# A chunked RWKV block and two attention layers on one core: top-128 selection with scores behind each query unit, masks made by GpSimd, and a new order of the steps in both attentions

## What is computed

```python
def block(args):                      # 128 queries
    s = jnp.einsum('bqhd,bsd->bqhs', qib, ki) * IDX_DIM ** -0.5      # 8 index heads
    score = jnp.einsum('bqh,bqhs->bqs', wib, jax.nn.relu(s))
    score = jnp.where(vis[None], score, NEG_INF)
    _, idx = lax.top_k(score, k_top)                                  # k_top = 128
    ...
    logits = jnp.einsum('bqgrd,bqkgd->bqgrk', qg, ksel) * scale + bias
    p = jax.nn.softmax(logits, axis=-1)
    o = jnp.einsum('bqgrk,bqkgd->bqgrd', p, vsel)
```

## Time and profile before

| | before |
|---|---|
| median of 3 runs | 2185.52 us (2184.66 to 2186.93) |
| the profiled execution | 2186.16 us |
| its span, first to last instruction | 2184.9 us |
| mean granted TensorE clock | 0.991 |
| first attention with selection | 810 to 1095 us |
| second attention | 1560 to 1780 us |

### The profile page before, as it was taken

One profiled execution on the slowest core, in us unless ns is written; L12 is line 12 of the kernel. 1 busy time (PEld: TensorE's weight loads), 2 busy tenths in 40 slices (PEclk: granted clock), 3 DMA queues, 4 the chain that ended last, 5 costly groups with the idle time before them and its releaser, 6 DMA issues.

```text
span 2184.9 us, 45350 instructions
## 1 busy us (share of the span) xinstructions
PE 2128.2 (97%) x19810; PEld 1871.8 (86%) x19810; DVE 1465.8 (67%) x2482; ACT 993.9 (45%) x1735; POOL 126.0 (6%) x121
## 2 busy tenths in 40 slices
PE   8999999999999999889999999999999999999999
PEld 2877788888778889778889999999988899999987
DVE  5889888887796866855576676334666567676622
ACT  4225556565525353245454444224666654443311
POOL 0000000000000004233310000000000030000000
PEclk9999999999999999979999999999999999999999
DMA  7631021111332543100132322223211023222232
GB/s 292 129 113 50 10 83 46 46 46 46 126 97 87 164 138 116 32 11 23 37 124 88 94 91 85 88 99 127 68 40 30 25 87 103 92 92 88 90 100 72
DMA packets 60021, 184.26 MB, mean 84 GB/s; under 512 B 7184, under 2 KB 11280, under 8 KB 59824
## 3 DMA queue, kind: packets, MB, share of 16 engines
q1 hardware_dynamic: 59824, 181.37, 25.8%
HBM read 174.73 MB, written 6.62 MB: 83 GB/s over the span
## 4 chain that ended last, share of the span: by engine, by line
PE 84%; DVE 10%; ACT 3%; issue 1%; DMA 1%; POOL 0%; SPq 0%; DVEq 0%; ACTq 0%
PE PS L604 67%; PE PS L789 3%; PE PS L778 2%; DVE ca L2064 2%; PE PS L1150 2%; PE PS L1281 2%; PE PS L798 1%; PE PS L1249 1%; DVE Swk L2501 1%; DVE mx L2497 1%; ACT Lb L1329 1%; DVE wlo L1962 1%; PE PS L1123 1%; PE PS L769 1%; DMA early<-in_wall 1%
## 5 line engine op out<-in xcount | busy, mean ns | idle before, releaser
L604 PE MATMUL PS<-nhi,whi 128*128 128x264 f32 (+1 forms) x2064 | 432.3, 291 | 2.4 <-ACT Vk L1329 1.5
L604 PE MATMUL PS<-nhi,wlo 128*128 128x264 f32 (+1 forms) x2064 | 419.1, 285 | 1.5 <-DVE wlo L1962 1.5
L604 PE MATMUL PS<-nlo,whi 128*128 128x264 f32 (+1 forms) x2064 | 419.3, 285 | 0.0
L1329 ACT ACTIVATE whi<-raw 128x1024 fp32r<-128x1024 f32 (+3 forms) x322 | 306.5, 953 | 199.5 <-PE PS L604 199.5
L1962 DVE TENSOR_TENSOR wlo<-raw,whi 128x1024 fp32r<-128x1024 f32 (+1 forms) x260 | 311.5, 1205 | 99.4 <-ACT whi L1329 99.3
L604 PEld LDWEIGHTS PS<-nhi,whi 128*128 128x128 f32 x2064 | 321.9, 191 | 9.9 <-ACT Vk L1329 1.7
L604 PEld LDWEIGHTS PS<-nhi,wlo 128*128 128x128 f32 x2064 | 321.3, 190 | 1.8 <-DVE wlo L1962 1.7
L604 PEld LDWEIGHTS PS<-nlo,whi 128*128 128x128 f32 x2064 | 321.7, 190 | 0.0
L604 PE MATMUL PS<-hhi,whi 128*128 128x512 f32 x648 | 266.5, 411 | 0.7 <-DVE hlo L2017 0.4
L604 PE MATMUL PS<-hhi,wlo 128*128 128x512 f32 x648 | 255.1, 394 | 0.5 <-DVE wlo L1962 0.4
L604 PE MATMUL PS<-hlo,whi 128*128 128x512 f32 x648 | 253.5, 391 | 0.0
(11 more groups left out here) (390 smaller groups left out, 3486.0 us busy)
## 6 DMA issues: line engine op xcount, KB each, us to landing
raw<-in_wall SPq DMA_DIRECT2D x266, 512.0 KB, 3.5
early<-in_wall SPq DMA_DIRECT2D x16, 512.0 KB, 14.7
raw<-in_wall SPq DMA_DIRECT2D x16, 384.0 KB, 3.0
TZ<-g_rows SPq DMA_DIRECT2D x2, 2112.0 KB, 10.0
raw<-in_wall SPq DMA_DIRECT2D x32, 128.0 KB, 2.0
raw<-in_wall SPq DMA_DIRECT2D x16, 256.0 KB, 2.7
g_rows<-gsb SPq DMA_DIRECT2D x8, 328.0 KB
xt<-in_xT SPq DMA_DIRECT2D x2, 1024.0 KB, 8.7
```

The costliest lines, as they stand in the source:

```text
L604: q = e.matmul(out, cuts[a][:, k * P:(k + 1) * P], (hi_, lo_)[b][:, kr, lo:lo + w], start=start and k == 0 and a == b == 0, stop=stop and ...
L1329: return e.activation(out, src, func, **kw)
```

## The change

Five things. The index products and scores of a query unit are done for all four blocks right behind that unit (t outside, i inside), in other PSUM banks (`SCORE_BANKS`), with two halves of `rel` in turn. The rounds write LOW into the scores themselves, the 16th round replaces too, and block 0 takes two rounds on the reversed negative scores; with that the mask is one comparison by GpSimd, and `above`, `equal`, `ranks`, `picked` and the sum of the masks are gone, as is the wait of a block's rounds for the mask of the block ahead. The scaling of a head's queries moves from VectorE to GpSimd (both norm gains go into the keys). In both attentions the steps behind a block of 528 keys have a new order: the result of the step ahead is applied and copied before the turn (first attention) or copied ahead of the scaling (second). `SELECT` is written anew with `FIRST` 5, and in `BEFORE` the letter p moves ahead of three t.

```diff
-BEFORE = "fftttpftfftptffffpfftftfffttfpffpffffftf"
+BEFORE = "ffptttftfftptffffpfftftfffttfpffpffffftf"
-SELECT = ("g" * 16 + 3 * "gggsggdggg" + "gsggdgrgrgrgrgr" + "grgrgrsgrgrdggg" + "sgrgrdgrsgrdgggg" + "sgrgrdgrgrgggg"
...
-FIRST = 4
+FIRST = 5
+SELECT = ("ggggggggggggggggggsggdsggsgggsgsgssgggdddddggsgsdddgggggsgddggssdggsdsdsggdsggrgrgrrgrgg"
...
+SCORE_BANKS = {3: ((4, 5), (6, 7)), 2: ((4,), (5,)), 1: ((6,), (7,)), 0: ((4,), (5,))}
...
         def tensor(e):
-                for i in (3, 2, 1, 0):
-                    q0, nq, w = rows_of(i)
-                    wide = w > 512
-                    for t in range(4):
+                for t in range(4):
+                    for i in (3, 2, 1, 0):
+                        q0, nq, w = rows_of(i)
...
+                    first = rest_apart(steps, n - 2)
+                    if first and n > 2:
+                        apply(n - 3)
+                    if not first and 2 <= n <= N + 1:
                         turn(n - 2)
                     yield
-                    if 3 <= n <= N + 2:
+                    if first:
+                        turn(n - 2)
...
         def scalar(e):
+                steps = [(t, i) for t in range(4) for i in (3, 2, 1, 0)]
+                for n, (t, i) in enumerate(steps):
                     w = WIDTH[i]
-                    for t in range(4):
-                        first = (4, 6) if w > 512 or t % 2 == 0 else (5, 7)
-                        for n in range(2):
-                            h = 2 * t + n
-                            on.wait_ge(*at("index", i, h))
-                            if h >= 4 or i < 3:
-                                on.wait_ge(*at("score", i if h >= 4 else i + 1, (h - 4) % 8))
-                            act(sv(rel[:, h % 4, 0:w], w), psv(w, first[n]), ACT.Relu, scale=0.125).then_inc(*up("rel", i, h))
-                        yield
+                    for r in range(2):
+                        h = 2 * t + r
+                        on.wait_ge(*at("index", i, h))
+                        if n > 1:
+                            before_t, before_i = steps[n - 2]
+                            on.wait_ge(*at("score", before_i, 2 * before_t + r))
+                        act(sv(rel[:, 2 * (n % 2) + r, 0:w], w), psv(w, SCORE_BANKS[i][r][0]), ACT.Relu,
+                            scale=0.125).then_inc(*up("rel", i, h))
+                    yield
...
                 for n in range(N + 6):
-                    if 1 <= n <= N:
+                    first = rest_apart(steps, n - 2)
+                    if not first and 1 <= n <= N:
                         weights(n - 1)
                     yield
                     if 3 <= n <= N + 2:
                         apply(n - 3)
+                    if first:
+                        weights(n - 1)
+                    if 3 <= n <= N + 2:
+                        squares(n - 3)
...
         def vector(e):
+                for n, (t, i) in enumerate((t, i) for t in range(4) for i in (3, 2, 1, 0)):
+                    w = WIDTH[i]
+                    for r in range(2):
+                        h = 2 * t + r
+                        on.wait_ge(*at("rel", i, h))
+                        made, wc = rel[:, 2 * (n % 2) + r, 0:w], wtok[:, i, h:h + 1]
+                        if h == 0:
+                            on.wait_ge(*at("wtok"))
+                            e.tensor_scalar(Ssc[i][:, :], made, wc, None, ALU.mult).then_inc(*up("score", i, h))
+                        else:
+                            on.wait_ge(*at("score", i, h - 1))
+                            e.scalar_tensor_tensor(Ssc[i][:, :], made, wc, Ssc[i][:, :], ALU.mult,
+                                                   ALU.add).then_inc(*up("score", i, h))
...
+                    left, many, n = Ssc[i][:, :], 16, 0
                     on.wait_ge(*at("score", i, 7))
-                    if i < 3:
-                        on.wait_ge(*at("mask_sum", i + 1))
                     e.memset(Ssc[i][0:64, w - 64:w], NEG).then_inc(*up("round", i, 0))
-                    src, many, thr, n = sc_, 16, mx8[:, 7:8], 0
                     if w == 144:
+                        left, many, n = Sneg[:, :], 2, 1
                         on.wait_ge(*at("round", i, 0))
-                        e.tensor_scalar(Swk[:, 0:w], sc_, -1.0, None, ALU.mult).then_inc(*up("round", i, 1))
-                        src, many, thr, n = Swk[:, 0:w], 3, cnt[:, 2:3], 1
+                        e.tensor_scalar(left, Ssc[i][:, ::-1], -1.0, None, ALU.mult).then_inc(*up("round", i, 1))
                     for r8 in range(many):
                         on.wait_ge(*at("round", i, n))
-                        e.max(mx8[:, :], src).then_inc(*up("round", i, n + 1))
-                        n += 1
-                        if r8 < many - 1:
-                            on.wait_ge(*at("round", i, n))
-                            e.match_replace(Swk[:, 0:w], mx8[:, :], src, LOW).then_inc(*up("round", i, n + 1))
-                            n += 1
-                            src = Swk[:, 0:w]
+                        e.max(mx8[:, :], left).then_inc(*up("round", i, n + 1))
+                        on.wait_ge(*at("round", i, n + 1))
+                        name = ("round", i, n + 2) if r8 < many - 1 else ("picked", i)
+                        e.match_replace(left, mx8[:, :], left, LOW).then_inc(*up(*name))
+                        n += 2
                         yield
-                    on.wait_ge(*at("round", i, n))
-                    if w == 144:
-                        e.tensor_scalar(thr, mx8[:, 0:1], -1.0, None, ALU.mult).then_inc(*up("round", i, n + 1))
-                        on.wait_ge(*at("round", i, n + 1))
-                    e.tensor_scalar(mask[i][:, :], sc_, thr, 0.0, ALU.is_gt, ALU.add,
-                                    accum_out=cnt[:, 0:1]).then_inc(*up("above", i))
-                    on.wait_ge(*at("above", i))
-                    e.tensor_scalar(cnt[:, 1:2], cnt[:, 0:1], -1.0, 128.0, ALU.mult, ALU.add)
-                    e.tensor_scalar(Swk[:, 0:w], sc_, thr, None, ALU.is_equal).then_inc(*up("equal", i))
-                    yield
-                    on.wait_ge(*at("equal", i))
-                    e.tensor_tensor_scan(sc_, onecol.broadcast_to([P, w]), Swk[:, 0:w], 0.0, ALU.mult,
-                                         ALU.add).then_inc(*up("ranks", i))
-                    on.wait_ge(*at("ranks", i))
-                    e.scalar_tensor_tensor(Swk[:, 0:w], sc_, cnt[:, 1:2], Swk[:, 0:w], ALU.is_le,
-                                           ALU.mult).then_inc(*up("picked", i))
-                    yield
...
         def gpsimd(e):
-                    for _ in range(nk - 1):
+                    q = count.next - first - 10
+                    for k in range(nk - 1):
+                        if 0 <= q < 8 and k == min(6, nk - 2):
+                            on.wait_ge(*at("qa_rs", q))
+                            e.tensor_tensor(qall[:, q, :], qall[:, q, :], sqh[:, 0:T], ALU.mult).then_inc(*up("qa", q))
...
-                    e.tensor_tensor(mask[i][:, :], mask[i][:, :], Swk[:, 0:w], ALU.add).then_inc(*up("mask_sum", i))
-                    on.wait_ge(*at("mask_sum", i))
-                    e.tensor_scalar(mask[i][:, :], mask[i][:, :], -1.0, -NEG, ALU.add, ALU.mult).then_inc(*up("mask_neg", i))
-                    on.wait_ge(*at("mask_neg", i))
+                    if w == 144:
+                        e.tensor_scalar(mask[i][:, :], Sneg[:, ::-1], 0.1 * LOW, NEG, ALU.is_lt, ALU.mult).then_inc(*up("mask_kept", i))
+                    else:
+                        e.tensor_scalar(mask[i][:, :], Ssc[i][:, :], 0.1 * LOW, NEG, ALU.is_gt, ALU.mult).then_inc(*up("mask_kept", i))
+                    on.wait_ge(*at("mask_kept", i))
```

More of the change, by code:

```diff
@@ L181 @@
     "dve_norm": "n0 x3_squares stats_0 stats_1 stats_meta",
-    "dve_a": "ki_raw wi qi score ka_raw round above equal ranks picked ka va qa_raw qa",
+    "dve_a": "ki_raw wi qi gains score ka_raw round picked ka va qa_raw",
     "dve_a_maps": "a_max a_neg a_inv a_PT oa",
@@ L574, in rest_at, with rest_apart @@
             return (6, w // P * P) if w < 512 else (7, 256)
+        def rest_apart(steps, n):
+            return 0 <= n < len(steps) and steps[n][1] == 3
         def attention_steps(first=0):
@@ L1748, in turn, with apply @@
                     act(pt[0:rem, whole, 0:nq], PS[0:rem, b, c0:c0 + nq], ACT.Copy).then_inc(*up("a_PT_act", n))
+                def apply(n):
+                    h, i = steps[n]
+                    q0, nq, w = rows_of(i)
+                    on.wait_ge(*at("a_applied", n))
+                    act(qall[:, h, q0:q0 + nq], PS[:, 7, 0:nq], ACT.Copy).then_inc(*up("a_o", n))
                 for n in range(N + 4):
                     yield
+                    first = rest_apart(steps, n - 2)
+                    if first and n > 2:
+                        apply(n - 3)
                     if n < N:
@@ L1757, in attend_a @@
```

(12 more changed lines are left out.)

67 lines of the change are left out of this document (29 added, 38 removed).

## The result

The changed kernel takes 2149.2 us (median of four runs, 2145.3 to 2151.7), the kernel before 2185.2: a ratio of 0.982, 95% interval 0.981 to 0.984. 2149.0 was forecast.

A forecast was written before the change was run, and what follows sets the result against it. TensorE, busy 2128.2 us, bounds the kernel; gains lie in its waits and low clock, with VectorE's list pacing 853 to 957 us. Terms 30 + 4.5 + 2.7 = 37.2 off 2186.2 give 2149 us; range 2141 to 2166.

The forecast's parts named there:

- The small terms: Outside the first attention's stage: `oT` copied ahead in the second attention, 4.5 us, and `BEFORE` reordered, 2.7 us.
- `BEFORE`: Near 160 us: with p ahead of three t, TensorE's wait at L733 goes; 2.7 us (0 to 2.9).
- The copy of `oT`: Second attention: copied ahead of ScalarE's scaling, it ends TensorE's waits at L1268; 4.5 us (0 to 4.9).
- The stage: First attention's stage: idle time and low clock won back, 36.2 us, less 4 and 2 given back: 30.
- the 4 that I gave back: 827 to 853 us: sums filled in ahead meet GpSimd instructions and wait for their end; 4 us lost (0 to 8).
- signs: First attention's stage: clock 1.00 throughout, VectorE above eight tenths busy from the first query unit, rounds ending some 25 us earlier.
- waits up to 2.9 us left the clock alone: TensorE's clock: only the three longest waits had low clock behind them, 12.9 us lost; shorter waits had none.
- That VectorE waits for GpSimd: First attention's stage: a VectorE sum in SBUF that meets a GpSimd instruction waits for its end; 4 us given back.
- the rival of exclusion throughout: VectorE and GpSimd exclude each other throughout: 4 us more ahead, 4 in the heads, 7.1 by low clock; 2164; chance 0.14.
- The start of the attention: 957 to 977 us: VectorE's shorter list ends L1150's 5.6 us wait and the low clock behind it; 5.3 + 7.1 us.
- The sum of list lengths: 853 to 957 us: VectorE's list sets the pace and shrinks by 29.4 us, from 104 to about 75, near TensorE's 80.

The follow-up runs named there:

- e0: The changed kernel run once more, with no edit, as the line the other runs are held against: 2151.0 us, ratio 0.983.
- the first two edits: Changed kernel with the old string `BEFORE`, 2152.5 us; changed kernel with the copy of `oT` behind the scaling in the second attention, 2154.4 us.
- e4: Changed kernel with VectorE also doing the old mask work once more, into tiles nobody reads: 2164.3 us, ratio 0.990.
- e8: Changed kernel with the old order of steps in the first attention on TensorE, ScalarE and VectorE: 2164.0 us, ratio 0.989.
- The two runs in the old order: Kernel before with masks and query scaling by GpSimd, sums and attention steps in old order: 2181.9 us; the same with rounds moved up: 2180.5 us.
- e5: Kernel before with the new rounds, masks and query scaling by GpSimd, old order of sums and steps, `FIRST` 4: 2181.9 us, ratio 0.998.
- e6: Changed kernel with GpSimd's eight scalings of H behind units 9 to 16 instead of 1 to 8: 2146.6 us.
- The last kernel: Changed kernel with scalings of H later, fifth index product two sub-steps later and four more `wlo` on VectorE: 2141.8 us, ratio 0.979.

## Why the prediction was right, and where it was not

**The small terms** held. `BEFORE`: 2.7 forecast, 2.3 by the wait, 1.5 and not clear of noise by the medians of the run that undoes it. The copy of `oT`: 4.5 forecast, 5.2 by the profile, 3.4 by the medians of the run that undoes it.

**The stage** was forecast at 30 and came to 33.2 in the profiled execution and in that of the repetition (e0). Two runs with the same stage (the first two edits, which lie outside it) show 275.4 and 275.5 us, so 30.1 to 30.2. The rounds, 102.8 us from first to last, came down to 78.8, about the 104 to 75 that I had worked out; the low clock went from between 853 and 977 us, and 4.8 us of new waits at the index products are the 4 that I gave back.

Not all signs came. The rounds end 9 us earlier and not 25. Counted from `kiT` they end 6.9 us earlier and start 17.1 later, behind the sums, and the attention's first step comes 36.8 us ahead of their end instead of 28.6. The 33.2 us are 15.1 up to the first `La`, 17.5 from there to the last, 0.6 behind it. So the selection is not finished 25 us sooner; TensorE has other work among the rounds. VectorE is busy for 66% and 54% of the two stretches from 828 to 865 us and not for eight tenths.

I had also read that waits up to 2.9 us left the clock alone. The kernel before has a fourth stretch of low clock, 3.4 us from 21.2 us on, behind waits of at most 2.0. And the new wait at the index product, 2.4 or 2.5 us long in eight profiled executions, is followed in all eight by 3.4 us or more of low clock, which begin within 2 us of its end, and in none of the three in which it is 1.7 us or less. The waits that I gave back had a price by the clock, an estimated 1.7 us, that I had put at nothing.

**That VectorE waits for GpSimd** was the reason for those 4. In the changed kernel, timelines of VectorE and GpSimd where the first sums stand:

```profile
828.25 2.47 DVE L2502 TENSOR_SCALAR Ssc<-rel,wtok 128x528 f32<-128x528 f32 x1 [2.50 <-ACT rel L1338]
...
834.76 2.02 DVE L2502 TENSOR_SCALAR Ssc<-rel,wtok 128x400 f32<-128x400 f32 x1
```

```profile
826.83 2.37 POOL L2824 TENSOR_TENSOR wlo<-raw,whi 128x1024 fp32r<-128x1024 f32 x1
...
834.18 2.37 POOL L2824 TENSOR_TENSOR wlo<-raw,whi 128x1024 fp32r<-128x1024 f32 x1 [3.75 <-ACT whi L1338]
```

They take 0.48 and 0.42 where no GpSimd instruction runs. The two runs that moved GpSimd's work away shortened the waits, and both together, with one product later, all but ended them. MAX8, MATCH_REPLACE8 and the evacuations from PSUM don't stretch: 528 wide, MAX8 has by the timeline a mean of 0.71 us in ten that met no GpSimd instruction and in six that did. Since those make up most of VectorE's list, the rival of exclusion throughout (2164) was rightly the lesser one.

**The step that failed** is in "The start of the attention": the 5.6 us wait of L1150 "came because the rounds of blocks 1 and 0 and their masks were still in VectorE's list ahead of what ScalarE needed. With VectorE 29 us shorter this goes". VectorE was late there, but most of the wait exists because a turn's last piece holds the apply's bank. With a long list and the new order of steps that line has 1.9 us (e4); with a short list and the old order it has 6.3 + 2.5 = 8.8 (e8), 2.2 at the longest, and the kernel loses 13.0 us. I gave the new order of steps no term of its own: undoing it costs as much as undoing the mask work. That the total was met nevertheless is in part luck: the stage's gain was credited to the list alone.

**The sum of list lengths** was right as a result, not as a rule. It says that masks and scaling by GpSimd would bring 22 to 30 us alone; they bring 4.7, although VectorE's list got shorter by nearly what was said. Undone one at a time from the changed kernel, the parts cost 13.3 (mask work), 13.0 (order of steps), 7.6 (scaling), 3.4 (`oT`) and 1.5 (`BEFORE`), 38.8 in all, more than the whole change brought (36.0) and without the order of the sums. So the parts lean on each other. The two runs in the old order, both within 7 us of before, lack the new order of the sums and that of the attention steps. The run with the old order of steps (e8) has the new sums alone on top of the masks and the scaling, with their string and `FIRST` 5: by the profiles the stage goes from 305.6 us before to 297.6 with masks and scaling (e5), to 286.9 with the new sums, and to 272.4 with the new order of steps. So masks and scaling bring 8.0, the sums another 10.7 and the steps another 14.5, in this order. It fits all runs that the shorter list pays only when no round trip over the index products stands between the rounds and no bank is held. What the new order of steps brings with the sums in the old order was not run.

**What the forecast did not have** is the spread of the result. See the last section.

## What to carry to other kernels

Compare lengths of lists to find the most a change can give, but price it by the round trips that stand in the busy stretch: TensorE to ScalarE to VectorE and back costs what stands ahead in each engine's list. VectorE's list got 16.1 us shorter in one run here and the stage only 8.0. When a wait has a releaser that is late, look at what makes TensorE need it at all, here a bank shared by two steps; undoing one part at a time shows it in a run. And do not let GpSimd's instructions with two inputs and VectorE's sums and products in SBUF meet in a stretch with such round trips.

## What the hardware showed unasked

The exclusion goes further than I said. A sum with one SBUF tensor and one scalar for each row (L2502, TENSOR_SCALAR) stretches as one with two tensors does, 2.47 us for 0.48, while MAX8 on the same tile does not. The Trainium skill (SBUF — State Buffer, "SBUF: two separate sides") names instructions in a two-port mode beside those with two SBUF inputs, which agrees as far as the stretching goes; that L2502 runs in such a mode no row says. But not every GpSimd instruction does this: in e4 a comparison by VectorE (TENSOR_SCALAR, 528 wide) took 0.48 us at 903.37 while GpSimd's comparison, with one tensor input, ran from 902.54 for 1.98. And a waiting VectorE instruction does not always get in between two of GpSimd: the `wlo` of 7.47 us waited through five.

Short stretches of low clock are one part of why one program takes 2145 or 2153 us. Windows of the run with the old string `BEFORE`, around the waits for `whi` (0.6 us) and `wlo` (1.5 us) near 1079 us:

```profile
1074.60:1080.20 5.60, 3.65 (x26) 3.04 (x25) 5.60 (x9) 5.12 (x9) 0.72 (x1) 1.00 0.72 243
1080.20:1086.60 6.40, 5.88 (x35) 5.88 (x36) 5.95 (x8) 2.50 (x4) 0.00 (x0) 0.73 0.52 164
```

In the profiled execution of the changed kernel the same waits, in the same place of the program, leave the clock at full, 2.4 GHz:

```profile
1069.00:1081.00 12.00, 9.10 (x68) 8.28 (x67) 12.00 (x18) 8.46 (x13) 1.45 (x2) 1.00 0.61 193
1081.00:1087.00 6.00, 6.00 (x49) 5.87 (x48) 2.54 (x5) 3.13 (x4) 0.00 (x0) 1.00 0.50 162
```

In the first of the two the granted clock is 0.51 from 1081 to 1083 us, the level of 1.2 GHz. From the last `La` to the first `flo` it is 46.3 us in the one and 44.8 in the other, so 1.5 us; from `kiT` to the first `La` another 1.4 (89.9 and 88.5). These are the two more stretches of 3.4 us that this execution has, near 1081 and near 866 us. I had taken waits of 2.9 us and less as harmless; here a few of 0.6 to 1.6 us are enough in some executions and not in others. What decides it I can't tell from these runs. The last kernel's profiled execution has the stretch near 1071 us too, and none near 840 and 865, where its waits are nearly gone; how much of its 9 us that is no run tells.

The other part lies ahead of the change. Up to `kiT` the ten profiled executions with the new string `BEFORE` run the same program, and `kiT` starts between 821.3 and 825.8 us. The one of e6 took 4.0 us more than that of the changed kernel, and 4.1 of them stand before `kiT` (825.6 and 821.5). Three of the ten, e6 among them, have a low clock at 21 us, and TensorE's waits that the profile puts down to nothing but issue, at L803 and L783, are 3.2 to 3.7 us in these three and 1.0 in the changed kernel's. Where those come from is open.
